# First modulation scales on TensorE and a place of their own for every first load: the head of a two-layer diffusion backbone

## What is computed

```python
mod = jax.nn.silu(cond) @ p['w_mod'][l] + p['b_mod'][l]
sh1, sc1, g1, sh2, sc2, g2, sh3, sc3, g3 = jnp.split(mod[:, None, :], N_MOD, axis=-1)
hf = rmsnorm(x, p['norm_pre'][l, 0]) * (1 + sc1) + sh1
f = swiglu(hf, p['ffn_w_gate'][l, 0], p['ffn_w_up'][l, 0], p['ffn_w_down'][l, 0])
x = x + 0.5 * g1 * rmsnorm(f, p['norm_post'][l, 0])
```

## Time and profile before

| | us |
|---|---|
| median of 3 runs | 3011.55 |
| lowest, highest | 3009.78, 3018.98 |
| the profiled execution, its own time | 3015.12 |
| its span | 3013.3 |
| PE busy | 2843.4 (94%) |
| DVE, ACT busy | 1784.2, 1104.9 |

### The profile page before, as it was taken

How to read it: one execution, slowest core, us unless ns; L and a number is a source line. 1 busy time by engine, 2 the same in 40 slices (tenths; PEclk the granted TensorE clock), 3 DMA queues, 4 the chain that set the end, 5 groups by cost and what they waited for, 6 DMA issues and landing times.

```text
span 3013.3 us, 47046 instructions
## 1 busy us (share of the span) xinstructions
PE 2843.4 (94%) x19310; PEld 2701.2 (90%) x19310; DVE 1784.2 (59%) x2643; ACT 1104.9 (37%) x1745; POOL 255.4 (8%) x197
## 2 busy tenths in 40 slices
PE   3999999997789999999999999999978899999997
PEld 2999999986579999999999999999944698999997
DVE  7566665755657555657665646457777747432334
ACT  3311114544766211136311226653333437211123
POOL 0000002000011000011000002000037611000002
PEclk7999999999999999999999999999999999999999
DMA  5445544421033544443543434522211133321233
GB/s 194 152 148 169 162 158 142 137 90 44 22 95 123 162 148 133 141 157 116 161 156 118 154 109 136 177 91 77 83 57 30 36 112 112 119 89 60 77 105 113
DMA packets 105175, 351.36 MB, mean 117 GB/s; under 512 B 11009, under 2 KB 27649, under 8 KB 104577
## 3 DMA queue, kind: packets, MB, share of 16 engines
q1 hardware_dynamic: 99328, 339.30, 35.5%
q10 hardware_dynamic: 5632, 9.05, 0.9%
HBM read 337.69 MB, written 10.62 MB: 116 GB/s over the span
## 4 chain that ended last, share of the span: by engine, by line
PE 84%; DVE 7%; ACT 3%; issue 3%; POOL 2%; DMA 1%; ACTq 0%; DVEq 0%; SPq 0%; POOLq 0%
PE P L1589 77%; PE P L1521 2%; DVE st L1166 1%; ACT pb L818 1%; DMA mraw<-wmod_d 1%; PE P L1835 1%; POOL mraw L631 1%; PE P L1757 1%; PE P L1613 1%; DVE wl L1044 1%; DVE xl L1084 1%; PE P L1800 1%; POOL toff L635 0%; DVE toff L1366 0%; DVE raw L1282 0%
## 5 line engine op out<-in xcount | busy, mean ns | idle before, releaser
L1589 PE MATMUL P<-xh,wh 128*128 128x320 f32 x4016 | 1021.2, 313 | 37.5 <-DVE xl L1084 31.6
L1589 PE MATMUL P<-xl,wh 128*128 128x320 f32 x4016 | 1006.4, 310 | 0.0
L1589 PE MATMUL P<-xh,wl 128*128 128x320 f32 x4016 | 1006.2, 310 | 0.0
L704 ACT CAST wh<-raw 128x1024 fp32r<-128x1024 f32 (+1 forms) x431 | 482.2, 1119 | 997.0 <-PE P L1589 801.3
L1589 PEld LDWEIGHTS P<-xh,wh 128*128 128x128 f32 x4016 | 696.8, 188 | 49.3 <-issue 33.8
L1044 DVE TENSOR_TENSOR wl<-raw,wh 128x1024 fp32r<-128x1024 f32 (+1 forms) x431 | 564.6, 1310 | 297.0 <-ACT wh L704 296.8
L1589 PEld LDWEIGHTS P<-xl,wh 128*128 128x128 f32 x4016 | 696.8, 188 | 2.8 <-issue 0.4
L1589 PEld LDWEIGHTS P<-xh,wl 128*128 128x128 f32 x4016 | 696.6, 188 | 0.0
L1589 PE MATMUL P<-hh,wh 128*128 128x320 f32 x1408 | 382.4, 312 | 0.0
L1589 PE MATMUL P<-hl,wh 128*128 128x320 f32 x1408 | 377.0, 308 | 0.0
L1589 PE MATMUL P<-hh,wl 128*128 128x320 f32 x1408 | 376.9, 308 | 0.0
(11 more groups left out here) (227 smaller groups left out, 2408.6 us busy)
## 6 DMA issues: line engine op xcount, KB each, us to landing
raw<-wgu_d SPq DMA_DIRECT2D x216, 512.0 KB, 3.9
mraw<-wmod_d SPq DMA_DIRECT2D x144, 512.0 KB, 3.6
raw<-wdB_d SPq DMA_DIRECT2D x64, 704.0 KB, 4.1
raw<-wdA_d SPq DMA_DIRECT2D x32, 704.0 KB, 5.5
raw<-ain_d SPq DMA_DIRECT2D x28, 512.0 KB, 3.5
raw<-sz_d SPq DMA_DIRECT2D x26, 512.0 KB, 3.9
raw<-sx_d SPq DMA_DIRECT2D x24, 512.0 KB, 3.5
raw<-aout_d SPq DMA_DIRECT2D x16, 512.0 KB, 3.6
```

Of the source, the lines that this page charges most:

```text
L704: nc.scalar.copy(wh[:, u.u % SPLITS, 0:n], raw[:, u.u % 2, 0:n]).then_inc(hi_done, 1)
L1589: ins = nc.tensor.matmul(P[:, u.banks[i], 0:C], w[:, u.u % SPLITS, k * 128:(k + 1) * 128], m[:, k, C * h:C * h + C], start=(k == 0 and w i ...
```

## The change

It touches the head alone.

- **Places.** The 8 shift tiles are loaded into `wshift`, the 8 scale tiles into `wscale`, each tile with a semaphore of its own, so SP issues all loads of the head in a row without a wait, those of `x` in two halves and those of units 0 and 1 among them. `wscale` lies where `xh` and part of `xl` come later.
- **Scales on PE.** `wscale` holds the weights as they are, input features on partitions. For each slice k the condition columns (`cond_cols`, 128x2, after Silu) stand in the array and 2 x 512 weights move (`scale`), which sums up two rows of 1024 in PSUM banks 4 and 5. ACT copies the rows into `scale_rows`, PE turns them back by 8 products with an identity, and DVE adds the bias straight from PSUM.
- **Conditions.** They arrive as one row of 2048 (8 KB) and PE spreads them by 4 products with `ones`; ACT's Silu reads PSUM. 1 MB of loads is gone.
- **First two units side by side.** PE takes units 0 and 1 slice by slice together (`first_units`). Half 1 of the head's norm moves into F0: `shifted`, `normed` and `lows` of half 1 come at places 2 to 9 (`FIRST_NORMED`), and the cast and subtraction of unit 2 come among the slices of half 0.

```diff
@@ sync
+            sp.dma_start(cond_rows[0:1, :], d["cond_rows"]).then_inc(rows_in, 16)
+            sp.dma_start(cond_cols[:, :, :], d["cond_cols"]).then_inc(cols_in, 16)
+            load_shift(0)
+            load_scale(0)
+            load_shift(1)
+            for dst, src in ((bmod[:, :, :], d["bmod"]), (npre[:, :, :, :], d["npre"]),
+                             (npost[:, :, :, :], d["npost"]), (cst[:, :], d["cst"])):
+                sp.dma_start(dst, src).then_inc(in_sem, 16)
+            load_x(0)
+            load_shift(2)
+            load_scale(1)
+            load_x(1)
+            for t in range(3, 6):
+                load_shift(t)
+                load_scale(t - 1)
+            load_scale(5)
+            load_shift(6)
+            load_scale(6)
+            load_unit(units[0])
+            load_scale(7)
+            load_shift(7)
+            load_unit(units[1])
@@ scalar
             for c in range(2):
-                nc.scalar.activation(sc[c][:, :], sc[c][:, :], ACT.Silu).then_inc(silu_c, 1)
-            act.wait_ge(in_sem, 16 * 5)
+                for q in range(2):
+                    act.wait_ge(cond_spread, 2 * c + q + 1)
+                    nc.scalar.activation(sc[c][:, 512 * q:512 * q + 512], P[:, 2 * c + q, :], ACT.Silu).then_inc(silu_c, 1)
...
             high(units[0])
+            for q in range(2):
+                act.wait_ge(scale_sum, 1)
+                nc.scalar.copy(scale_rows[0:2, 512 * q:512 * q + 512], P[0:2, 4 + q, :]).then_inc(scale_cp, 1)
             high(units[1])
-            for h in range(2):
-                for k in range(KD):
-                    shifted(0, h, k)
+            for k in range(KD):
+                shifted(0, 0, k)
+                if k == KD - 3:
+                    high(units[2])
@@ vector
-            dve.wait_ge(silu_c, 2)
-            for t in range(FIRST_MODS):
+            for t in range(KD - 1):
                 mod_tile(t)
-            dve.wait_ge(in_sem, 16 * 5)
+            low(units[0])
+            mod_tile(KD - 1)
+            low(units[1])
...
             pre_factor(0)
-            low(units[0])
-            low(units[1])
-            for h in range(2):
-                for k in range(KD):
-                    normed(0, h, k)
-                    if k:
-                        lows(0, h, k - 1)
-                lows(0, h, KD - 1)
+            for k in range(KD):
+                normed(0, 0, k)
+                if k:
+                    lows(0, 0, k - 1)
+                if k == KD - 2:
+                    low(units[2])
+            lows(0, 0, KD - 1)
...
+                if where == "F0" and not s and i in FIRST_NORMED:
+                    normed(0, 1, FIRST_NORMED[i])
+                    if FIRST_NORMED[i]:
+                        lows(0, 1, FIRST_NORMED[i] - 1)
@@ tensor
+            def first_units(us):
+                for u in us:
+                    pe.wait_ge(lo_done, u.u + 1)
+                for k in range(KD):
+                    pe.wait_ge(xn_ready[0], k + 1)
+                    for u in us:
+                        ins = products(u, k, xh, xl)
+                        if k == KD - 1:
+                            ins.then_inc(unit_done, 1)
...
+            def scale(k):
+                pe.wait_ge(scale_in[k], 16)
+                for b in range(2):
+                    ins = mm(P[0:2, 4 + b, :], cond_cols[:, k, :], wscale[:, k, 512 * b:512 * b + 512], start=(k == 0), stop=(k == KD - 1))
+                if k == KD - 1:
+                    ins.then_inc(scale_sum, 1)
+
+            pe.wait_ge(rows_in, 16)
+            for q in range(4):
+                mm(P[:, q, :], ones[0:1, :], cond_rows[0:1, 512 * q:512 * q + 512], start=True, stop=True).then_inc(cond_spread, 1)
+            pe.wait_ge(cols_silu, 1)
+            scale(0)
             for h in range(2):
-                for k in DIRECT[PRE]:
+                for k in range(KD):
                     total(PRE, 0, h, k)
+                scale(h + 1)
+            for k in range(3, KD):
+                scale(k)
+            pe.wait_ge(scale_cp, 2)
+            pe.wait_ge(in_sem, 16 * 4)
+            pe.wait_ge(silu_c, 4)
+            for t in range(KD):
+                ins = mm(P[:, 3, 2 * t:2 * t + 2], scale_rows[0:2, 128 * t:128 * t + 128], ident[0:2, 0:2], start=True, stop=True)
+            ins.then_inc(scale_tr, 1)
+            first_units(units[0:2])
```

More of the change, by code:

```diff
@@ L311, in build @@
         in_sem = sem("in_sem")
+        x_in = [sem("x_in0"), sem("x_in1")]
+        rows_in = sem("rows_in")
+        cols_in = sem("cols_in")
+        cond_spread = sem("cond_spread")
+        cols_silu = sem("cols_silu")
+        shift_in = [sem("shift_in%d" % t) for t in range(KD)]
+        scale_in = [sem("scale_in%d" % t) for t in range(KD)]
+        scale_sum = sem("scale_sum")
+        scale_cp = sem("scale_cp")
+        scale_tr = sem("scale_tr")
         hi_done = sem("hi_done")
@@ L510, in build @@
         NORMED = {0: {4: (0,), 5: (1,), 6: (2,), 7: (3,)}, 1: {6: (0,), 7: (1,), 8: (2,), 9: (3,)}}
+        FIRST_NORMED = {2 + k: k for k in range(KD)}
         POST_TOTAL = {0: (0, 4), 1: (0, 5)}
@@ L980, in _ @@
                     window0(s, i, (p.name, s))
+                if where == "F0" and not s and i in FIRST_NORMED:
+                    shifted(0, 1, FIRST_NORMED[i])
                 if where == "F0" and s:
@@ L1436, in _ @@
                     window1(s, i)
-                if where == "F1" and i == 0 and s:
-                    lows(s, 1, KD - 2)
+                if where == "F0" and not s and i in FIRST_NORMED:
+                    normed(0, 1, FIRST_NORMED[i])
+                    if FIRST_NORMED[i]:
+                        lows(0, 1, FIRST_NORMED[i] - 1)
+                if where == "F1" and i == 0:
+                    if s:
+                        lows(s, 1, KD - 2)
                     lows(s, 1, KD - 1)
-                if u.u + 2 < len(units):
+                if 2 < u.u + 2 < len(units):
                     low(units[u.u + 2])
@@ L1553, in window1, with products @@
                     total(PRE, s, 1, k)
+            def first_units(us):
[7 more added lines that the diff above has]
+                            ins.then_inc(unit_done, 1)
+            def products(u, k, rh, rl):
+                for w, m in ((wh, rh), (wh, rl), (wl, rh)):
+                    for i, h in enumerate(u.hs):
+                        ins = nc.tensor.matmul(P[:, u.banks[i], 0:C], w[:, u.u % SPLITS, k * 128:(k + 1) * 128],
+                                               m[:, k, C * h:C * h + C],
+                                               start=(k == 0 and w is wh and m is rh),
+                                               stop=(k == u.p.nk - 1 and w is wl))
+                return ins
             def unit(u):
@@ L1586, in unit @@
                                 window1(s, (u.place[1], tenth))
[L1587 to L1592 removed]
+                    ins = products(u, k, rh, rl)
                 ins.then_inc(unit_done, 1)
```

83 lines of the change are left out of this document (53 added, 30 removed).

## The result

| | before | changed |
|---|---|---|
| median, us | 3011.55 | **2984.34** |
| lowest to highest, us | 3009.78 to 3018.98 (4 runs) | 2981.58 to 2985.15 (4 runs) |
| the profiled execution, us | 3015.12 | 2983.99 |

The ratio is 0.9901, 95% interval [0.9889, 0.9913]: 29.8 us less, from 26.2 to 33.4 (the medians alone differ by 27.2), and more than the 0.3% that a measurement tells from no change. The forecast was 2984.0 in a range from 2978 to 3000. The same kernel a second time took 2987.16 against 3011.82 (ratio 0.9909 [0.9892, 0.9926]).

A forecast was written before the change was run, and what follows sets the result against it. PE, 94% busy, was taken as the bound, so only its early waits could be won: 77.1 - 48.3 - 1.0 = 27.8 us, giving 2987.3 against the profiled execution, 2984 for the median; range 2978 to 3000.

The forecast's parts named there:

- last step: End of the sum: the profiled execution before lay 3.6 us above its median, so 2987.3 became 2984 for the median.
- Bound now: First 65 us: PE waits while modulation tiles pass through two buffers and DVE, 5.92 us per two tiles, 50 us for 16.
- Effective start: When PE would start its units if run back to back at full clock: 77.1 us before, 48.3 after, plus 1 for waits.
- Transfers: Head loads: 365 GB/s for large ones, 9.2 us for x; unit 1's weights land at 39.8, scale tile 7 at 36.9.
- The last scale product: End of the scales on PE: 1.7 us after its tile lands, at 38.6 us.
- TensorE's products: New PE work: 0.85 us per full-precision product at full clock; spreading 3.4 to 6.8 us, done by 10.1; turning back 16 passes.
- Behind it: After the scales: two ACT copies to 39.9, unit 1's cast 41.0, subtraction 42.3, factor 43.0; PE starts at 45.1 us.
- First two units: Units 0 and 1 together, paced by DVE's 1.16 us slices, done at 55.3 us; the 4.73 us wait before unit 2 goes.
- Rival A: Scale products run at the lower clock: +8.3 us, 2992, or about +16, 3000, with spreading and sums slow too; chance 0.22.
- Rival B: In F0, the second half's normalization delays subtractions and PE waits anew, 8 us together: 2992; chance 0.08.
- Rival C: Load queue stays at 165 GB/s, unit 1 lands 39.3 us later, kernel takes 3023; break-even 195 GB/s; chance 0.04.
- Rival D: Every bound on its bad side: 354 GB/s, 2 us lag, 4.5 us of lower clock; 5.3 us less gain, 2989; chance 0.08.

The follow-up runs named there:

- scales twice: Changed kernel with PE doing scale tiles 2 to 7 a second time into banks nothing reads; median 2996.34 us, 0.9941 of the kernel before.
- half 2's sums late: Changed kernel with the eight sums of squares of the second token half behind the scales, its root later; 2985.34 us, 0.9909 of the kernel before.
- places alone: Kernel before with only a place for every load of the head; DVE scales, loaded conditions, units 0 and 1 sequential; 3003.79 us, ratio 0.9966.
- units in turn: Changed kernel with units 0 and 1 one after the other again, half 1's norm ahead of unit 2's cast; 2994.42 us, 0.9944 of the kernel before.
- side by side alone: Kernel before with only units 0 and 1 slice by slice and half 1 of the first norm in F0; 3008.25 us, ratio 0.998.
- scales on DVE: Changed kernel with the scale tiles multiplied on DVE again, each in its own place; 3000.64 us, 0.9961 of the kernel before.
- two more loads: Changed kernel with two unused loads of 0.72 MB each behind the second half of x; 2987.94 us, 0.991 of the kernel before.

## Why the prediction was right, point by point

**The forecast held by its mechanism and by luck in its last step.** It said a head 27.8 us shorter; the traces show 30.24. It then took off another 3.6 us, for the profiled execution of before against its median. The changed kernel's profiled execution had no such excess (2983.99 at a median of 2984.34), so by the forecast's sum that execution should have taken 2987.3, and took 3.3 less, 2.4 of it in the head and the rest behind it. The two misses cancel. The medians alone could not tell: their interval, 26.2 to 33.4 us, holds both 27.8 and 30.24.

- **Bound now**: right. The round trip through two buffers and DVE went, and PE's three long waits with it.
- **Effective start before, 77.1; after, 48.3 and 1 us for small waits, 49.3**: unit 2 starts at 53.89 without a wait, less 48 x 0.147 = 46.85. The step is 2.4 us off: the first product was 1.4 us early, and the 1 us of small waits did not come.
- **Transfers, the term most off.** 365 GB/s for large loads; measured 408 to 412. 286 for x, from a store in the same pieces; measured 382 to 390. By these 9.44 MB take 23.0 us instead of 25.9 and x 6.8 instead of 9.2: 5.3 us in all. The first loads ran lower (352 GB/s in the window from 4 to 8 us), so the landings are about 4 us early: x's second half at 19.13 (21.1), scale tile 7 at 33.20 (36.9), unit 1's weights at 35.72 (39.8). The 286 was a misreading: its window of 3 us reaches past the end of the store. Inside the store the kernel before moves 362 GB/s, by which x would have been put at 7.2 us:

```profile
3010.00:3012.00 2.00, 0.00 (x0) 0.00 (x0) 0.00 (x0) 0.00 (x0) 0.00 (x0) 0.50 1.05 362
```

  The 1.0 us from the last byte to the semaphore stood in no row either. In the changed kernel's trace x's last packet ends at 18.62 and unit 1's at 35.30, 0.5 and 0.4 us ahead of their landings.
- **The last scale product at 38.6, bound by its landing**: it ended at 37.5, bound by PE. This step's cause was wrong, and scales twice shows it: 10.45 us where a landing-bound chain had room. Its size was right within 1.1 us, because the forecast's two limits lay close: PE's own, six tiles of 1.7 us from 26.5, ends at 36.7, and the landing's at 38.6. By the measured landing of tile 7 (33.20) the second would have been 34.9.
- **TensorE's products**: 0.85 a pass at half clock and 0.43 at full one, as taken from the earlier trace rows. The spreading took 7.16 us, done at 9.7 (3.4 to 6.8, done by 10.1). The turning back took 1.94 us against 2.4.
- **Behind it**: two copies 1.05 us together (1.2), unit 1's cast in the queue behind them as named, subtraction, factor done at 41.37 (43.0), first product 2.4 us after it (2.1). Start 43.73 instead of 45.1.
- **First two units**: 10.16 us from the first product to unit 2's start, predicted 10.2. The half clock there, 5.8 us long, cost nothing, since the slices set the pace: with half 2's sums late PE has the full clock there, and unit 2 starts 12.7 us behind `ga` in both.
- **Rival A, scales at the lower clock (0.22)**: refuted by the block of 10.46 us. Products with 2 output columns held the full clock through all of it. Of the price named, the spreading, scale 0 and the first four of the sums' passes ran slow: these start 0.53 to 0.69 us apart from 13.50 on, the later ones 0.27. The first half's sums took 6.43 us against the second's 5.45, so about 1 us of the rival's 16 came true, an estimate.
- **Rival B, a new wait in F0 (0.08)**: refuted, PE has no wait between 43.73 and 100 us. It exists one step further on: half 2's sums late ran into it at unit 3.
- **Rival C, a slow queue (0.04)**: refuted, 410 GB/s against its break-even of 195. The 165 to 203 of before were two buffers' turns.
- **Rival D**: none of its bounds came on the bad side. The first products did run at the lower clock, but PE lost nothing by it.

On the transfers two places of the Trainium skill differ. The Trainium skill, "DMA: Bandwidth & Descriptors", Specifications, has about 358 GB/s from HBM for a core; the windows of 408 to 412 GB/s, over 14 us, lie 14 to 15% above it, so that rule is not this kernel's limit. The Trainium skill, "Perfetto Trace Analysis", Roofline, says that a core whose neighbour is idle can draw more than its share, up to some 435 GB/s of its 16 DMA engines; the measured rates agree with that. By 435 GB/s the 9.44 MB would be 21.7 us, an estimate, 1.3 less than by the measured rate.

The Trainium skill, "TensorE: Matmul & The Clock Gate", Part 1, which the prediction cited, says that the throttled state is the default. The trace agrees: PE's very first products took 0.85 a pass, twice the later 0.43.

## What to carry to other kernels

When a head is a round trip of buffer, transfer and engine, cost each engine's whole work as a floor before you price the removal of the wait: places alone gave 9.9 us, not the 20 that the transfers would have allowed, because DVE had 41.5 us of its own to do. Even with that floor counted 15 were expected; the floor began 1.3 us later, a tile cost 2.45 us instead of 2.34, and 2.65 us of waits came on top. Work that is put on an engine which waits anyway is free only until it becomes the chain: ask of a new product both when its operand lands and when its engine gets to it, and give the later. To move work behind the new chain, follow what else waits for that work: eight sums moved well, and their root with its table loads gave all of it back until it was moved too.

## What was not expected

- **A deep queue of loads runs at 408 to 412 GB/s** with 512 KB loads, and at 382 to 390 while x's pieces of 1280 bytes are in it too, while one load at a time in each of two buffers had given 165 to 203.
- **The clock column can be wrong at the start.** It shows 1.00 from 0 to 16 us, while twelve passes of 512 columns up to 13 us took 0.85 and more each, the pace of 1.2 GHz in the earlier trace rows. The trace's first clock record stands at 15.53 us, in the middle of the first sums, where the passes get fast; ahead of its first record the column shows 1.00 all the same. In such a place the time of one pass is the better clock.
- **The rest of the program is not constant.** The span less the head is 2844.4 before and 2843.6 changed, 2843.05 with units in turn, 2843.35 and 2842.5 with places and side by side alone, yet 2851.5 with scales on DVE and 2850.5 with two more loads, all with the same instructions past the head. In the trace of scales on DVE 6.5 us of the 8 arise between 2150 and 2400 us, the scan, and 6.1 of them in two steps: from PE's wait at 2275.09 to that at 2303.88 it takes 28.79 us, the changed kernel for the same work 25.79 (2265.78 to 2291.57), and the next round has 28.83 against 25.77. In both the granted clock is at 0.50 for some 6 us that run at 1.00 in the changed kernel; two more loads has the same two steps. The first of them, scales on DVE and then changed:

```profile
2275.00:2281.00 6.00, 5.91 (x15) 3.69 (x16) 1.76 (x6) 2.77 (x5) 1.02 (x2) 0.50 0.15 44
```

```profile
2266.00:2272.00 6.00, 6.00 (x30) 3.17 (x30) 3.66 (x7) 3.76 (x7) 2.19 (x2) 1.00 0.16 44
```

  PE had waited just before for 2.61 us in the one and 2.62 in the other, so the wait alone doesn't say where the clock falls. The changed kernel's own runs spread over 9.7 us in the last series. Why the clock falls behind a wait in one kernel and not behind the same wait in another stays open; no run here set it on purpose.
